# One-hot rows for expert 0, a list made before its first product, and gate and up weights in 4 KB runs, in a one-core mixer and mixture-of-experts kernel

## The reference

```
h   = rms_norm(x, norm1_g);  proj = h @ w_in
mix = concat(window attention with sinks, silu(gb) * group_norm(retention))
x   = x + mix @ w_out
h2  = rms_norm(x, norm2_g)
p_group = softmax(h2 @ rg_w + rg_b);  g_prob, g_idx = top_k(p_group, 1)
sel = (h2 @ re_w + re_b)[group g_idx];  top_p, top_i = top_k(softmax(sel), 2)
w   = g_prob * top_p / sum(top_p)
out = sum over e of combine[:, e] * ((silu(h2 @ w_gate[e]) * (h2 @ w_up[e])) @ w_down[e])
return rms_norm(x + out, final_norm_g)
```

## Time and profile before

| | |
|---|---|
| median of 3 runs | 553.96 us (551.9 to 554.74) |
| the profiled execution | 551.27 us |
| its span in the trace | 549.5 us |
| PE busy | 535.5 us, 97% of the span |
| DVE, ACT, POOL busy | 421.5, 353.6, 92.6 us |
| DMA moved | 144.03 MB, mean 262 GB/s |

### The profile page before, as it was taken

One profiled execution on the slowest core, in us unless ns is written; L12 is line 12 of the kernel. 1 busy time (PEld: TensorE's weight loads), 2 busy tenths in 40 slices (PEclk: granted clock), 3 DMA queues, 4 the chain that ended last, 5 costly groups with the idle time before them and its releaser, 6 DMA issues.

```text
span 549.5 us, 7877 instructions
## 1 busy us (share of the span) xinstructions
PE 535.5 (97%) x2662; PEld 437.4 (80%) x2663; DVE 421.5 (77%) x580; ACT 353.6 (64%) x473; POOL 92.6 (17%) x113
## 2 busy tenths in 40 slices
PE   7999999999999999999999999999999999999995
PEld 4988777777877888877788888888888888888883
DVE  5654599555864753588989898988989898988996
ACT  5553664780326253355778978788778978788745
POOL 3260000000000000031412222022212222110620
PEclk9999999999999999999999999999999999999998
DMA  8999112323020237649999999999999999999996
GB/s 321 374 306 396 30 66 78 76 79 78 0 78 0 78 114 253 226 146 321 349 381 375 376 393 383 347 340 359 390 370 369 375 395 369 368 395 393 323 210 203
DMA packets 63821, 144.03 MB, mean 262 GB/s; under 512 B 3833, under 2 KB 13361, under 8 KB 63665
## 3 DMA queue, kind: packets, MB, share of 16 engines
q1 hardware_dynamic: 56528, 120.24, 61.9%
q0 software_dynamic: 7120, 22.90, 13.8%
q10 hardware_dynamic: 144, 0.52, 0.2%
HBM read 132.77 MB, written 14.30 MB: 268 GB/s over the span
## 4 chain that ended last, share of the span: by engine, by line
PE 88%; DVE 5%; ACT 2%; DMA 2%; issue 2%; POOL 0%; DVEq 0%; POOLq 0%
PE ps L1507 25%; PE ps L1509 24%; PE ps L1508 24%; PE ps L1514 7%; PE ps L1658 2%; PE ps L1644 2%; PE ps L1620 1%; PE ps L1590 1%; PE ps L1685 1%; DMA arena<-norm_g 1%; DMA arena<-h_dram,meta 1%; DVE lo_ring L1317 1%; PE ps L1911 1%; DVE act_lo L1027 1%; DVE res L1486 0%
## 5 line engine op out<-in xcount | busy, mean ns | idle before, releaser
L1317 DVE TENSOR_TENSOR lo_ring<-arena,hi_ring 128x2048 fp32r<-128x2048 f32 x94 | 213.9, 2289 | 26.8 <-ACT hi_ring L894 26.7
L1507 PE MATMUL ps<-hi_ring,act_hi 128*128 128x512 f32 x576 | 229.8, 399 | 1.5 <-DVE lo_ring L1317 1.1
L1509 PE MATMUL ps<-hi_ring,act_lo 128*128 128x512 f32 x576 | 224.9, 390 | 0.0
L1508 PE MATMUL ps<-lo_ring,act_hi 128*128 128x512 f32 x576 | 224.4, 390 | 0.0
L894 ACT ACTIVATE hi_ring<-arena 128x2048 fp32r<-128x2048 f32 x94 | 180.1, 1916 | 28.1 <-PE ps L1509 28.1
L1507 PEld LDWEIGHTS ps<-hi_ring,act_hi 128*128 128x128 f32 x576 | 108.2, 188 | 23.5 <-issue 2.4
L1509 PEld LDWEIGHTS ps<-hi_ring,act_lo 128*128 128x128 f32 x576 | 108.1, 188 | 23.3
L1508 PEld LDWEIGHTS ps<-lo_ring,act_hi 128*128 128x128 f32 x576 | 108.4, 188 | 21.0
L1017 DVE SCALAR_TENSOR_TENSOR lo_ring<-arena,over,hi_ring 128x512 fp32r<-128x512 f32 x40 | 29.3, 748 | 29.4 <-ACT hi_ring L709 29.2
L1027 DVE TENSOR_TENSOR act_lo<-ps,act_hi 128x512 fp32r<-128x512 f32 x56 | 36.7, 684 | 7.0 <-ACT act_hi L742 5.1
L600 POOL DMA_INDIRECT arena<-h_dram,gather_idx x14 | 34.6, 2473 | 24.0 <-issue 24.0
(11 more groups left out here) (239 smaller groups left out, 524.2 us busy)
## 6 DMA issues: line engine op xcount, KB each, us to landing
arena<-w_gate SPq DMA_DIRECT2D x32, 1024.0 KB, 16.7
arena<-w_up SPq DMA_DIRECT2D x32, 1024.0 KB, 18.0
arena<-w_down SPq DMA_DIRECT2D x32, 1024.0 KB, 15.5
arena<-w_in SPq DMA_DIRECT2D x16, 512.0 KB, 6.4
y_dram<-arena POOLq DMA_DIRECT2D x8, 512.0 KB, 10.7
res<-y_dram POOLq DMA_DIRECT2D x8, 512.0 KB, 9.7
arena<-w_in SPq DMA_DIRECT2D x2, 1024.0 KB, 11.0
arena<-w_out SPq DMA_DIRECT2D x4, 512.0 KB, 6.2
```

The lines of the kernel that those rows point to most:

```text
L1317: nc.vector.tensor_tensor(lo(N1 + n12), raw(n12), hi(N1 + n12).bitcast(F32), ALU.subtract).then_inc(lo_done, 1)
L1507: nc.tensor.matmul(dst, a_hi, b_hi, start=start, stop=False)
L1508: nc.tensor.matmul(dst, a_hi, b_lo, start=False, stop=False)
L1509: return nc.tensor.matmul(dst, a_lo, b_hi, start=False, stop=stop)
```

## The change

Rows for expert 0 come from a matmul. `h2` of all four token tiles stays in the arena (`h2_home`) and DVE makes, for each tile, a one-hot matrix `first_hot` of who stands where in expert 0's list, from the rank counts straight away (`find_first`). PE multiplies each h2 tile with it, which gives the gathered rows already transposed (`first_rows`: 4 float32 matmuls of 128 columns for each tile and half, 32 in all). `keep_clock` is gone from this stretch. The lists are made in one pass ahead of the first product. `list_fields` for the routing weights moves behind the two first products. POOL gathers whole lists for experts 1, 2 and 3.

Part of DVE's work moves: the exponents' differences go to POOL, lengths, slots and flags into expert 0's `step`; the prefix sum of the flags is made only where lists overflow. ACT makes the high part of granule 2 ahead of the rows. SP's loads of slots 8, 9 and 10 wait for the last write of `h2`, for half of the rows of expert 0, and for the gather of expert 1.

The gate and up weights are loaded with two neighbouring rows on a partition, in runs of 4 KB where they were 2 KB, and so all transposes of token rows read their columns with a step of two (`row_cols`).

```diff
-        w_gate_v = w_gate.rearrange("a e (k p) n -> (a e) p k n", p=P)
+        w_gate_v = w_gate.rearrange("a e (h g p j) n -> (a e) p h g (j n)", h=2, g=2, p=P)
@@ SP @@
-                if n == RING2 - 4:
-                    sp.wait_ge(rows_in[0], 16)
+                if n == O_BIAS // GRAN - 1:
+                    sp.wait_ge(h2_out[T - 1], 16)
+                elif n == O_BIAS // GRAN:
+                    sp.wait_ge(x_turned, 1)
+                elif n == O_BIAS // GRAN + 1:
+                    sp.wait_ge(rows_in[1], 16)
@@ POOL @@
+            pool_done(nc.gpsimd.tensor_tensor(diff.rearrange("p t g j -> p (t g j)"), route[:, 704:768], route[:, 640:704], ALU.subtract))
+            pool_done(nc.gpsimd.tensor_tensor(diff, diff, lg[:, :, 1:, :], ALU.mult))
...
+            for n in (8, 4, 2):
+                pool_done(nc.gpsimd.tensor_tensor(folded[:, :, 0:n], folded[:, :, 0:n], folded[:, :, n:2 * n], ALU.add))
...
             pool.wait_ge(lists_ready, 1)
-            for b in range(2):
-                pool.indirect_dma_start(x_rows[b], None, h2_dram, bass.IndirectOffsetOnAxis(ap=meta[:, 4 * b:4 * b + 1], axis=0),
-                                        bounds_check=last_token, oob_is_err=False).then_inc(rows_in[b], 16)
+            pool.wait_ge(x_turned, 2)
+            gather_whole(1)
+            gather_whole(2)
@@ ACT @@
             split(2, 2, 16)
-            rows_hi(0, 1)
+            nc.scalar.activation(stat[:, 46:47], eps[:, 0:1], ACT.Exp)
+            rows_hi(0, 1, (0,))
+            act.wait_ge(gate_d, 1)
+            nc.scalar.activation(route[:, 848:868], route[:, 848:868], ACT.Exp).then_inc(gate_e, 1)
+            rows_hi(0, 1, (1,))
@@ DVE @@
+            def find_first(t0, t1, ahead):
+                last = t1 == T
+                step_done(nc.vector.tensor_scalar(miss[:, t0:t1], standing[:, t0:t1, 0, 0], 2.0, 2.0 * S, ALU.is_ge, ALU.mult))
+                dve.wait_ge(rank_ready, 2 if last else 1)
+                step_done(nc.vector.tensor_tensor(first_rank[:, t0:t1], ahead, miss[:, t0:t1], ALU.add))
+                for t in range(t0, t1):
+                    nc.vector.tensor_scalar(first_hot[:, t, :], order, first_rank[:, t:t + 1], None,
+                                            ALU.is_equal).then_inc(first_hot_set, 1)
...
+            find_first(0, EARLY, ps[:, 1, 0:EARLY * E:E])
             find_ranks(0, EARLY, ps[:, 1, 0:EARLY * E])
-            mark(0)
             norm2(T - 1)
             gate(EARLY, T)
-            mark(1)
+            find_first(EARLY, T, ps[:, 2, 0:(T - EARLY) * E:E])
             find_ranks(EARLY, T, ps[:, 2, 0:(T - EARLY) * E])
-            for t in range(EARLY, T):
+            for t in range(T):
                 mark(t)
+            rows_lo(0, 1, (0,))
+            for piece in range(2):
+                split_piece(N1 + 1, piece)
             dve.wait_ge(lists_made, 1)
...
+            rows_lo(0, 1, (1,))
+            for piece in range(2, 4):
+                split_piece(N1 + 1, piece)
...
             split(2, 2)
+            split(3, 3)
...
+            def step(b, e, last=False, first=False):
                 for c in range(PER_E):
+                    if c == 1 and first and b == 0:
+                        set_hid(e)
                     split(e * PER_E + 4 + c, (4 + PER_E * b + c) % RING2)
+                    if first and c == 0 and b == 0:
+                        rows_lo(1, 3)
+                    if first and c == 4 and b == 0:
+                        set_slots()
+                    if first and c == 5 and b == 0:
+                        set_flags()
...
                     if c == 2:
                         row_lo(hid_t[1], 6, hid_t[0], hid_hi, e + 1, hid_lo)
+                        if first and b == 0:
+                            set_lengths()
@@ PE @@
+            def row_cols(a, i):
+                c0 = 4 * a * P + i // 2 * 2 * P + i % 2
+                return slice(c0, c0 + 2 * P - 1, 2)
+            def first_rows(t, a):
+                pe.wait_ge(h2_ready, t + 1)
+                pe.wait_ge(first_hot_set, t + 1)
+                for i in range(4):
+                    ins = nc.tensor.matmul(ps[:, 4 + a, i * P:(i + 1) * P], h2_home[t][:, row_cols(a, i)],
+                                           first_hot[:, t, :], start=(t == 0 and i == 0), stop=(t == T - 1 and i == 3),
+                                           skip_group_check=True)
+                return ins
-            keep_clock(3, 0)
+            first_rows(0, 0)
             logits(2 * T - 1)
+            first_rows(0, 1)
+            first_rows(1, 0)
...
+            first_rows(1, 1)
+            for a in range(2):
+                first_rows(2, a)
+                first_rows(3, a).then_inc(x_turned, 1)
...
-            keep_clock(21, 0)
...
-            pe.wait_ge(rows_in[0], 16)
-            for a in range(2):
-                turn(4 + a, [x_rows[0][:, (4 * a + i) * P:(4 * a + i + 1) * P] for i in range(4)]).then_inc(x_turned, 1)
+            pe.wait_ge(x_lo, 1)
+            product(0, xt[0], 0, 0, 0, True, False, first=True)
+            pe.wait_ge(x_lo, 2)
+            product(0, xt[0], 4, 1, 1, False, True)
             pe.wait_ge(weights_set, 2)
             for t in range(T):
                 ins = list_fields(3, 2, t, t == 0, t == T - 1)
             ins.then_inc(weights_made, 1)
-            product(0, xt[0], 0, 0, 0, True, False)
-            product(0, xt[0], 4, 1, 1, False, True)
```

More of the change, by code:

```diff
@@ L217, in build @@
         gain1_col, gain2_col = gain_cols[:, 0:KD], gain_cols[:, KD:2 * KD]
-        h2_buf = [region(O_XG, D), region(O_XG + D, D)]
+        x_rows = [region(O_XG, D), region(O_XG + D, D)]
+        h2_home = [region(O_BIAS, D), region(O_BIAS + D, D), x_rows[1], x_rows[0]]
+        first_hot = region(O_BIAS + 2 * D, T * P).rearrange("p (t s) -> p t s", t=T)
         gain2 = region(O_GAIN, D)
@@ L450, in load_expert @@
                 else:
-                    sp.dma_start(as_chunks(raw(slot)), w[kind][e][:, 4 * half:4 * half + 4, :]).then_inc(w2_in[slot], 16)
+                    sp.dma_start(as_chunks(raw(slot), 2 * SEG), w[kind][e][:, half, :, :]).then_inc(w2_in[slot], 16)
             def kind_of(s):
@@ L894, in split, with rows_hi @@
                 nc.scalar.activation(hi(N1 + n12), raw(n12), ACT.Copy).then_inc(hi_done, 1)
-            def rows_hi(b, wait):
-                for a in range(2):
+            def rows_hi(b, wait, halves=range(2)):
+                for a in halves:
                     act.wait_ge(x_turned, wait + a)
@@ L1391, in _, with set_lengths @@
-            nc.vector.tensor_copy(over[:, UNITS + 1:2 * UNITS + 1], flags[cur]).then_inc(over_set, 1)
-            def step(b, e, last=False):
+            def set_lengths():
+                step_done(nc.vector.tensor_scalar(quarters, count, float(QUARTER), None, ALU.is_gt))
+                for i in (2, 3):
+                    step_done(nc.vector.scalar_tensor_tensor(quarters, count, float(QUARTER * i), quarters,
+                                                             ALU.is_gt, ALU.add))
+                nc.vector.tensor_copy(meta_v[:, :, 3:4], quarters.unsqueeze(2)).then_inc(lengths_made, 1)
@@ new lines, in _, with set_flags @@
+            flags, any_flag = r(0, UNITS), r(64, 1)
+            def set_flags():
+                for i in range(1, S // P):
+                    ins = nc.vector.tensor_scalar(flags[:, (i - 1) * E:i * E], count, float(P * i), None, ALU.is_gt)
+                step_done(ins)
+                nc.vector.tensor_copy(over[:, 0:UNITS], flags)
+                step_done(nc.vector.tensor_reduce(any_flag, flags, AX_X, ALU.add))
+                nc.vector.tensor_copy(over[:, 2 * UNITS:2 * UNITS + 1], any_flag).then_inc(over_set, 1)
@@ new lines, in number_flags @@
+            def number_flags():
+                sums = [region(9 * GRAN + 64 * i, UNITS) for i in range(2)]
+                step_done(nc.vector.tensor_scalar(sums[0], over[:, 0:UNITS], 0.0, None, ALU.add))
+                for n in range(6):
+                    a, b = sums[n % 2], sums[1 - n % 2]
+                    nc.vector.tensor_copy(b[:, 0:1 << n], a[:, 0:1 << n])
+                    step_done(nc.vector.tensor_tensor(b[:, 1 << n:], a[:, 1 << n:], a[:, 0:UNITS - (1 << n)], ALU.add))
+                step_done(nc.vector.memset(over[:, UNITS:UNITS + 1], 0))
+                nc.vector.tensor_copy(over[:, UNITS + 1:2 * UNITS], sums[0][:, 0:UNITS - 1]).then_inc(over_set, 1)
@@ L1401, in step @@
                     if c == 2:
                         row_lo(hid_t[1], 6, hid_t[0], hid_hi, e + 1, hid_lo)
+                        if first and b == 0:
+                            set_lengths()
                     if c == 3 and not last:
                         rows_lo(b, e * 2 + 5)
-            split(3, 3)
-            rows_lo(1, 3)
-            with dve.Fori(0, E // 2 - 1) as q:
+            for e in range(2):
+                step(e, e, first=True)
+            with dve.Fori(1, E // 2 - 1) as q:
```

(9 more changed lines are left out.)

173 lines of the change are left out of this document (79 added, 94 removed).

## The result

The changed kernel takes 549.51 us (median of 5 runs, 549.0 to 549.66), the kernel before 552.15 us (median of 5). The ratio is 0.9939 with a 95% interval of 0.9916 to 0.9961: 0.6%, or 2.6 us, faster. Of 75 further executions of the kernel before, 21 took over 553.5 us and most others 551 to 552.5, and two of the three shown ahead of the prediction are of the longer kind.

A forecast was written before the change was run, and what follows sets the result against it. PE, busy 97% of the span, was taken as the bound, with the gain in the routing. 4.25 - 0.95 + 1.38 - 1.0 gave 3.7 us off the 553.96 median: 550.3 us, range 547.3 to 554.5.

The forecast's parts named there:

- DVE's debt: Expert 0's step: moved lengths, slots and flags keep DVE busy, so PE loses 1.0 us before granules 8 to 10 (bounds 0, 2.0).
- The new front: Routing: expert 0's rows from matmuls instead of the gather, first product at 246.1 in place of 250.36, 4.25 us earlier.
- the logits keep their start: Routing on PE: late logits still start at 237.25, as they wait for ACT's copy; no cost.
- Lists between products: Behind the first products: the weights' lists, formerly ahead of the first product, now cost PE 0.95 us.
- rows of expert 1: Gather issued at 247.2, landed at 253, PE asks at 255.25: no cost; upper end 1.9 us. Late-rows rival shared chance 0.18.
- stall before granule 4: Expert 0: PE's wait of 1.28 us from 262.26 to 263.54, and 0.1 behind it, gone: 1.38 us gained.
- The step of two: I take none: PE's strided stationary loads in transposes and `first_rows`: taken at no cost, the lower bound.
- the upper bound of 18.5: Strided PE loads at half speed: 18.5 us more, so 568.8 us as a rival, chance 0.08.
- 4 KB runs and SP at nothing: Gate and up weight loads: longer runs and SP's changed waits cost nothing, since loads are ahead of use.
- The DMA as a bound: Long middle of the experts: loads set the pace, so the time stays at 554.0 us; chance 0.04.
- The clock: Routing and first products: without idle matmuls PE could drop to 1.2 GHz, giving 554 us; rival with chance 0.02.

The follow-up runs named there:

- sorted: The changed kernel with 4 KB runs kept but even and odd columns of the normalized rows stored apart, so PE reads without a step: 548.36 us, ratio 0.9923.

## Why the prediction was right, and where it was not

The predicted time, 550.3 us, is 0.8 us above the measured one. It stood on a saving of 3.7 us from a median of 553.96, and both were too high: the saving is 2.6 (medians of 5), and the base 552.15. The two errors cancel in part, which is luck: 3.7 us off 552.15 would have been 548.45. What holds is the sign and the stretches; by its own steps, on the trace's clock:

| step | predicted | measured |
|---|---|---|
| first product | -4.25 (246.1) | 246.87; see below, -4.0 to -4.3 |
| from there to `hid` of expert 0 | +0.95 - 1.38 = -0.4 | 15.66 for 15.99, -0.3 |
| expert 0 to 1, DVE's debt | +1.0 | 18.65 for 17.67, +1.0 |
| experts 1 to 13 | 0 | 212.80 for 212.24, +0.6 |
| from expert 13 to the start of DVE's last operation | 0 | 49.10 for 48.95, +0.15 |
| from there to the span's end | 0 | 4.62 for 4.29, +0.3 |

**The new front: right.** The two profiled executions differ by 3.49 us at the first product, but the changed one was 0.63 us late already at the logits ahead of the routing (235.39 for 234.76), before the one-hot rows begin. That is scatter: these logits lie between 234.68 and 235.60 in the profiles of the old front and between 235.23 and 235.58 in those of the new. Over all profiles the six kernels with the old front have the first product at 250.95 on average (250.36 to 251.48), the four with the new one and the step at 246.95, the three without the step at 246.57. That is 4.0 us with and 4.4 without the step, around the 4.25 that was worked out. Counted from those logits, the first product comes after 15.60 to 15.99 us (mean 15.76) with the old front, 11.49 with the new one and 11.21 without the step: 4.3 and 4.5 us sooner. One premise did not hold: "the logits keep their start" relative to what is ahead. They come 2.75 us behind the ones before them (235.39 to 238.14), where the kernel before has 2.49 (234.76 to 237.25), because `first_rows(0, 0)` starts only at 237.13. The late ranks come 0.15 us later too (5.82 us behind the earlier logits for 5.67). The 40 records on the path took 0.1175 us each, not 0.11 by the 0.88 for a group of eight (and sorted 0.112: 4.48 us for the 40, 241.24 to 245.72).

**Lists between products, rows of expert 1, stall before granule 4: right.** The weights' lists cost 0.81 us (252.43 to 253.24) for 0.95. Expert 1's rows cost PE nothing, with the issue at 248.2 where 247.2 was predicted and the landing at about 252.85 where 253 was taken. The kernel without the hold shows what that rested on: 1.3 us. The stall is gone, by the order on DVE as the working had it (granule 4's low part, then the rows of expert 1), and by the flags no longer standing in front of ACT's silu, which the working did not name; on the kernel before it took both to end it.

**DVE's debt: right, the size with some luck.** 1.0 us was the forecast, 0.98 came (18.65 less 17.67), in pieces before granules 8, 9 and 10, though the profile names DVE at one of them alone. The mechanism held: DVE ran without a break from `hid` to granule 10's low part, 18.1 us as worked out (260.07 to about 278.2). But 259.05 + 18.1 is 277.15 and not the 277.4 of the working, so by its own terms the debt was 0.7. What made up for the slip is that `hid` began 13.20 us behind the first product (246.87 to 260.07), where 12.95 was worked out. A second slip is in the sum: 281.29 less 277.45 is 3.84, and the parts give 3.7, which was taken.

**The step that failed is "The step of two: I take none".** It costs about 1.2 us: 549.55 less 548.36, or 0.9 between the two spans. The mechanism considered was the right one (loads of the stationary operand), the lower bound was taken as the value, and the upper bound of 18.5 was 15 times too far out. The rows show how the term is made up: 66 ns more for a transpose's load, of which 11 ns reach PE's pace, and 4 ns more for a record's load, with PE's pace 5 ns slower (0.1175 for 0.112). With 120 transposes and 64 records, 40 of them on the path, that is an estimate of 120 x 0.011 + 40 x 0.005 = 1.5 us. On the traces it is 0.28 us up to the first product (11.49 less 11.21) and about 0.05 in each expert's step; why the steps take less than 0.09 is not shown. The list pass, the nearest row, was a moving operand and told nothing of this one. Had the term been in, the sum would have been a saving of 2.5, near the 2.6 and 2.3 (551.86 less 549.55) of the medians; but taken from 553.96 it would have given 551.5 us, further from 549.5 than the 550.3 that was forecast.

The rule of the Trainium skill that was weighed there (page "SBUF — State Buffer", section "Door 1: The DMA port swizzle": lines of 16 bytes, full bandwidth from two hits on a line) fits the records, 192, 196 and 329 ns at steps of one, two and four, since at a step of four floats each line is hit once. It does not fit the transposes, 141, 207 and 208 ns. There the measurement decides: two hits on a line are not free for a transpose's load.

**4 KB runs and SP at nothing: right.** With the DMA at 393 instead of 374 GB/s nothing ends sooner. The DMA as a bound, the rival with 0.04, is refuted from both sides: more rate brings nothing, and the kernel with 2 KB runs and the new front has the whole gain. The Trainium skill, page "DMA: Bandwidth & Descriptors", section "Where 436 GB/s comes from", gives about 358 GB/s as a core's limit from HBM. With one core running the traces do not agree: 374 GB/s were held for 200 us before, and 393 now.

**The clock: right.** It was granted in full from 237 to 281 us without the idle matmuls, and again from 300 to 500 (1.00 in each stretch above).

**The end is 0.3 us longer**, from the start of DVE's last operation to the span's end, in all profiles with the new front (4.6 to 4.7) against 4.3 to 4.4 in those with the old. No experiment was made on it. It stays open.

## What to carry to other kernels

When an operand of an operation is addressed in a new way and no row shows that operand so, the lower bound is the wrong value to take: put in a small price for each instruction and count the instructions (here 11 ns by 120), or sort the data where an engine with slack writes it, as the norm on DVE did here at no cost (1.28 us for a tile of 1024 columns either way). A stall can have two holders of about equal length, so ask of each wait what would end last once its releaser is early. Work moved off the path onto an engine that is 90% busy is paid when it next falls due: here 1.0 us, and moving it one step further won back only 0.3 on the trace.

## What was not expected of the hardware

- A float32 weight load with a step costs a transpose and a plain matmul differently: 141, 207, 208 ns at steps of one, two, four for the transpose; 192, 196, 329 ns for the record of a plain matmul, with PE's pace at 0.112, 0.1175 and 0.233 us a record.
- A pause of about 1 us on PE was followed by some 4 us at 1.2 GHz in the profile of the kernel without the running sum, and not in others with the same pause; with the pause halved, none of 12 executions was long. That the pause is the cause is likely and not shown.
- PE's idle matmuls were dropped and replaced by work, and the granted clock stayed at 1.00 from 236 to 256 us in the changed kernel. With a step of four it fell to 0.50 from 242 to 244 us though PE was busy all the time, behind loads of 329 ns; the records' pace did not change with it.
